# Transposes of the FFN activations: 32-bit float against the rounded 32-bit type, one unit later, in other PSUM banks

## What is computed

```python
hn = rms_norm(h, ffn_norm[i])
h = h + (jax.nn.silu(hn @ w_gate[i]) * (hn @ w_up[i])) @ w_down[i]     # D_FF = 5632
```

## Time and profile before

| | |
|---|---|
| median of 3 runs | 1308.03 us (1307.72 to 1308.03) |
| the profiled execution | 1307.81 us, its span 1306.1 us |
| TensorE busy | 1299.4 us (99%), granted clock at full speed throughout |
| VectorE busy | 1038.9 us (80%) |
| ScalarE busy | 713.9 us (55%) |
| bytes moved | 238 MB, mean 183 GB/s |

### The profile page before, as it was taken

How to read it: one execution, slowest core, us unless ns; L and a number is a source line. 1 busy time by engine, 2 the same in 40 slices (tenths; PEclk the granted TensorE clock), 3 DMA queues, 4 the chain that set the end, 5 groups by cost and what they waited for, 6 DMA issues and landing times.

```text
span 1306.1 us, 18433 instructions
## 1 busy us (share of the span) xinstructions
PE 1299.4 (99%) x6589; PEld 1073.9 (82%) x6589; DVE 1038.9 (80%) x1366; ACT 713.9 (55%) x946; POOL 57.1 (4%) x71
## 2 busy tenths in 40 slices
PE   9999999999999999999999999999999999999998
PEld 7788888888888888888888888888888888888887
DVE  6578885788586668999888977679888987968784
ACT  6576444544455556655455654445555545555753
POOL 5003000221000000000000000000000000000000
PEclk9999999999999999999999999999999999999999
DMA  8555544555444555766566656666666556657554
GB/s 272 177 177 162 160 148 130 146 147 148 144 128 145 178 177 162 219 216 185 184 200 204 204 188 208 187 211 188 195 208 211 188 181 210 191 178 221 181 180 162
DMA packets 126204, 238.37 MB, mean 183 GB/s; under 512 B 9711, under 2 KB 10786, under 8 KB 126138
## 3 DMA queue, kind: packets, MB, share of 16 engines
q1 hardware_dynamic: 126106, 237.48, 58.5%
q10 hardware_dynamic: 32, 0.01, 0.0%
HBM read 235.36 MB, written 2.10 MB: 182 GB/s over the span
## 4 chain that ended last, share of the span: by engine, by line
PE 97%; DVE 2%; ACT 0%; DMA 0%; issue 0%; DVEq 0%; ACTq 0%
PE pair L653 15%; PE pair L655 15%; PE pair L654 15%; PE pair L934 12%; PE pair L936 12%; PE pair L935 12%; PE bg L934 2%; PE bg L936 2%; PE bg L935 2%; PE bg L774 2%; PE bg L844 2%; PE bg L711 1%; PE bg L929 1%; DVE w_lo L1582 1%; PE bg L825 0%; PE bg L686 0%
## 5 line engine op out<-in xcount | busy, mean ns | idle before, releaser
L1582 DVE TENSOR_TENSOR w_lo<-raw,w_hi 128x1024 fp32r<-128x1024 f32 x442 | 532.8, 1222 | 163.8 <-ACT w_hi L1162 162.0
L1162 ACT ACTIVATE w_hi<-raw 128x1024 fp32r<-128x1024 f32 x399 | 415.3, 1055 | 246.5 <-PE pair L655 116.2
L653 PE MATMUL pair<-w_hi,xT_hi 128*128 128x512 f32 x716 | 289.5, 404 | 0.2 <-DVE w_lo L1847 0.2
L655 PE MATMUL pair<-w_hi,xT_lo 128*128 128x512 f32 x716 | 280.1, 391 | 0.0
L654 PE MATMUL pair<-w_lo,xT_hi 128*128 128x512 f32 x716 | 279.4, 390 | 0.0
L655 PEld LDWEIGHTS pair<-w_hi,xT_lo 128*128 128x128 f32 x716 | 134.4, 188 | 29.0
L653 PEld LDWEIGHTS pair<-w_hi,xT_hi 128*128 128x128 f32 x716 | 134.6, 188 | 27.1 <-issue 0.6
L654 PEld LDWEIGHTS pair<-w_lo,xT_hi 128*128 128x128 f32 x716 | 134.8, 188 | 24.7
L934 PE MATMUL pair<-w_hi,actT_hi 128*128 128x512 f32 x296 | 115.8, 391 | 0.0
L936 PE MATMUL pair<-w_hi,actT_lo 128*128 128x512 f32 x296 | 115.3, 390 | 0.0
L935 PE MATMUL pair<-w_lo,actT_hi 128*128 128x512 f32 x296 | 115.2, 389 | 0.0
(11 more groups left out here) (385 smaller groups left out, 1939.3 us busy)
## 6 DMA issues: line engine op xcount, KB each, us to landing
raw<-in_w_in_dram SPq DMA_DIRECT2D x112, 512.0 KB, 3.8
raw<-in_w_gate_dram SPq DMA_DIRECT2D x88, 512.0 KB, 4.2
raw<-in_w_up_dram SPq DMA_DIRECT2D x88, 512.0 KB, 4.2
raw<-in_w_down_dram SPq DMA_DIRECT2D x88, 512.0 KB, 4.8
raw<-in_w_o_dram SPq DMA_DIRECT2D x32, 512.0 KB, 4.5
raw<-in_w_ple_gate_dram SPq DMA_DIRECT2D x32, 512.0 KB, 4.8
raw<-in_w_ple_proj_dram SPq DMA_DIRECT2D x4, 512.0 KB, 4.4
h<-in_x_dram SPq DMA_DIRECT2D x3, 512.0 KB, 8.0
```

The costliest lines, as they stand in the source:

```text
L653: mm(banks[t][:], hi[:, ts], wh, start=first, stop=False)
L655: m = mm(banks[t][:], lo[:, ts], wh, start=False, stop=last)
L1162: f(w_hi[j % RING][:], raw[j % RING][:], ACT.Copy).then_inc(hi_ready, 1)
L1582: v.tensor_tensor(w_lo[j % RING][:], raw[j % RING][:], w_hi[j % RING][:].bitcast(F32), ALU.subtract).then_inc(lo_ready, 1)
```

## The change

The product of VectorE now goes to `gate_s` in place. ScalarE issues two DMAs that copy it, bits unchanged, into `act_r`, a tensor of the rounded type at the place of `act_s`. TensorE waits for their landing, transposes `act_r` against an identity of the rounded type (`ident_r`), and does so behind unit 3 instead of unit 2, into `bg[2]` and `bg[3]`. In `mixed_units` the product of `bg[2]` goes last and has the wait for `actT_lo`; `t_hi` and `t_lo` are made in pieces of 1 and 2 thirds instead of 2 and 1. The copying out of the banks stands behind the split of unit 6, outside `split_mixed`. `p1` is held in `v_s` instead of `act_s[1]`, and two VectorE instructions change places.

```diff
+TURN_BEHIND = 3
...
+        act_r = [sb(f"act_r{t}", [P, CB], F32R, at=mix + (52 + 2 * t) * KIB) for t in range(NT)]
...
+        ident_r = sb("ident_r", [P, P], F32R)
...
+            def tp_r(out, in_):
+
+                return nc.tensor.transpose(out.bitcast(F32R), in_, ident_r[:])
...
-            def turn_act():
-
-
+            def turn_act(n):
+
+                pe.wait_ge(ident_ready, 1)
+                for t in range(NT):
+                    pe.wait_ge(act_moved[t], n * 16)
                 for q in range(2):
                     for kk in range(2):
                         for t in range(NT):
                             cs = slice((2 * q + kk) * P, (2 * q + kk + 1) * P)
-                            m = tp(bg[q][:, kk * TOK + t * P:kk * TOK + t * P + P], act_s[t][:, cs], ident[:])
+                            m = tp_r(bg[2 + q][:, kk * TOK + t * P:kk * TOK + t * P + P], act_r[t][:, cs])
                     m.then_inc(ff_full[q], 1)
...
-                pe.wait_ge(t_lo_ready, n)
-                product(bg[2][:], F_hi[:, q, 2, :], F_lo[:, q, 2, :], t_hi[:, 1, :], t_lo[:, 1, :], first, last)
+                pe.wait_ge(t2_lo_ready, n)
                 product(bg[1][:], F_hi[:, q, 0, :], F_lo[:, q, 0, :], t_hi[:, 0, :], t_lo[:, 0, :], first, last)
-                pe.wait_ge(t4_lo_ready, n)
+                pe.wait_ge(t34_lo_ready, n)
                 product(pair[0][1][:], xT_hi[:, k1, a1], xT_lo[:, k1, a1], t_hi[:, 2, :], t_lo[:, 2, :], False,
-                        last).then_inc(t_used, 1)
+                        last)
+                if turned is not None:
+                    for f in range(2):
+                        pe.wait_ge(ff_free[f], turned)
+                product(bg[2][:], F_hi[:, q, 2, :], F_lo[:, q, 2, :], t_hi[:, 1, :], t_lo[:, 1, :], first, last).then_inc(t_used, 1)
...
-                            if not peeled:
-                                for n in range(2):
-                                    pe.wait_ge(ff_free[n], i + n0)
...
-                    if j == 2 and not peeled:
+                    if j == TURN_BEHIND and not peeled:
                         pe.wait_ge(pair_free[1], i * 2 + b0)
                         pe.wait_ge(gate_sum, i * 2 + 2 * n0)
-                        turn_act()
+                        turn_act(i + n0)
...
+            act.wait_ge(consts_ready, 1)
+            f(ident_r[:], ident[:], ACT.Copy).then_inc(ident_ready, 1)
             post("gains", 0)
...
-                f(t_hi[:, 0:2, :], t_raw[:, 0:2, :], ACT.Copy).then_inc(t_hi_ready, 1)
-                f(t_hi[:, 2, :], t_raw[:, 2, :], ACT.Copy).then_inc(t_hi_ready, 1)
+                f(t_hi[:, 0, :], t_raw[:, 0, :], ACT.Copy).then_inc(t_hi_ready, 1)
+                f(t_hi[:, 1:3, :], t_raw[:, 1:3, :], ACT.Copy).then_inc(t_hi_ready, 1)
...
+            def move_act(freed):
+
+                act.wait_ge(pair_free[1], freed)
+                for t in range(NT):
+                    act.dma_start(act_r[t][:].bitcast(F32), gate_s[t][:]).then_inc(act_moved[t], 16)
...
-                        split_mixed(u, j + LEAD, i * len(MIXED) + (m0 + q + 1), peeled and n0 == 0 and q == 0,
-                                    None if peeled or q else lambda: turned(i + (n0 - 1), i * 4 - 4))
+                        split_mixed(u, j + LEAD, i * len(MIXED) + (m0 + q + 1), peeled and n0 == 0 and q == 0)
                     else:
                         split(u, j + LEAD)
+                    if j == TURN_BEHIND and not peeled:
+                        turned(i + (n0 - 1), i * 4 - 4)
...
+                    if j == 0 and not peeled:
+                        move_act(i * 2 + b0)
                     if j == mixed_end:
                         act.wait_ge(t_used, i * len(MIXED) + (m0 + len(MIXED)))
-                        f(act_s[1][:], bg[0][:], ACT.Copy).then_inc(p1_copied, 1)
+                        f(v_s[:], bg[0][:], ACT.Copy).then_inc(p1_copied, 1)
...
-                v.tensor_tensor(t_lo[:, 0:2, :], t_raw[:, 0:2, :], t_hi[:, 0:2, :].bitcast(F32),
-                                ALU.subtract).then_inc(t_lo_ready, 1)
+                v.tensor_tensor(t_lo[:, 0, :], t_raw[:, 0, :], t_hi[:, 0, :].bitcast(F32),
+                                ALU.subtract).then_inc(t2_lo_ready, 1)
                 dve.wait_ge(t_hi_ready, 2 * n)
-                v.tensor_tensor(t_lo[:, 2, :], t_raw[:, 2, :], t_hi[:, 2, :].bitcast(F32),
-                                ALU.subtract).then_inc(t4_lo_ready, 1)
+                v.tensor_tensor(t_lo[:, 1:3, :], t_raw[:, 1:3, :], t_hi[:, 1:3, :].bitcast(F32),
+                                ALU.subtract).then_inc(t34_lo_ready, 1)
...
-                        v.tensor_tensor(v_s[:], bg[1][:], p1[:], ALU.subtract).then_inc(v_ready, 1)
-                        v.tensor_tensor(gate_s[0][:], pair[0][0][:], p1[:], ALU.add).then_inc(gate_sum, 1)
+                        v.tensor_tensor(gate_s[0][:], pair[0][0][:], v_s[:], ALU.add).then_inc(gate_sum, 1)
+                        v.tensor_tensor(v_s[:], bg[1][:], v_s[:], ALU.subtract).then_inc(v_ready, 1)
...
-                            v.scalar_tensor_tensor(out=act_s[t][:], in0=up[:], scalar=h_rs[0][:, t:t + 1],
+                            v.scalar_tensor_tensor(out=gate_s[t][:], in0=up[:], scalar=h_rs[0][:, t:t + 1],
```

More of the change, by code:

```diff
@@ L382, in build @@
         h1_copied = sem("h1_copied")
+        act_moved, ident_ready = [sem(f"act_moved{t}") for t in range(NT)], sem("ident_ready")
         act_copied, act_form, act_rounded, down_sum = (
@@ L387, in build @@
         t1_ready, t2_ready, t34_ready = (sem(f"t{n}_ready") for n in (1, 2, 34))
[L388 to L389 removed]
+        t_hi_ready, t2_lo_ready, t34_lo_ready, t_used = (
+            sem(n) for n in ("t_hi_ready", "t2_lo_ready", "t34_lo_ready", "t_used"))
         p1_copied, gate_sum, v_ready, up_sum = (
@@ L936, in product, with mixed_units @@
                 return mm(o, lo, wh, start=False, stop=last)
-            def mixed_units(u, j, q, n):
+            def mixed_units(u, j, q, n, turned=None):
                 first, last = q == 0, q == len(MIXED) - 1
@@ L1046, in down @@
                                     False).then_inc(unit_used, 1)
-                            pe.wait_ge(t_lo_ready, count)
-                            product(bg[2][:], D_hi[:, q, 2, :], D_lo[:, q, 2, :], t_hi[:, 1, :], t_lo[:, 1, :], first, last)
+                            pe.wait_ge(t2_lo_ready, count)
                             product(bg[1][:], D_hi[:, q, 0, :], D_lo[:, q, 0, :], t_hi[:, 0, :], t_lo[:, 0, :], first, last)
-                            pe.wait_ge(t4_lo_ready, count)
+                            pe.wait_ge(t34_lo_ready, count)
                             product(pair[0][1][:], actT_hi[:, k1, a1], actT_lo[:, k1, a1], t_hi[:, 2, :], t_lo[:, 2, :], False,
-                                    last).then_inc(t_used, 1)
+                                    last)
+                            product(bg[2][:], D_hi[:, q, 2, :], D_lo[:, q, 2, :], t_hi[:, 1, :], t_lo[:, 1, :], first, last).then_inc(t_used, 1)
                             continue
@@ L1107, in _ @@
                             False).then_inc(unit_used, 1)
-                    pe.wait_ge(t_lo_ready, MIX_PG + q + 1)
-                    product(bg[2][:], E_hi[:, q, 3, :], E_lo[:, q, 3, :], t_hi[:, 1, :], t_lo[:, 1, :], first, last)
+                    pe.wait_ge(t2_lo_ready, MIX_PG + q + 1)
                     product(bg[1][:], E_hi[:, q, 1, :], E_lo[:, q, 1, :], t_hi[:, 0, :], t_lo[:, 0, :], first, last)
-                    pe.wait_ge(t4_lo_ready, MIX_PG + q + 1)
+                    pe.wait_ge(t34_lo_ready, MIX_PG + q + 1)
                     product(pair[0][1][:], xT_hi[:, k1, a1], xT_lo[:, k1, a1], t_hi[:, 2, :], t_lo[:, 2, :], False,
-                            last).then_inc(t_used, 1)
+                            last)
+                    product(bg[2][:], E_hi[:, q, 3, :], E_lo[:, q, 3, :], t_hi[:, 1, :], t_lo[:, 1, :], first, last).then_inc(t_used, 1)
                     continue
@@ L1443, in split_mixed @@
                 f(w_hi[j % RING][:], raw[j % RING][:], ACT.Copy).then_inc(hi_ready, 1)
-                if between:
-                    between()
                 if not n0_first:
@@ L1533, in _ @@
                     gate_up(i, ug, bgt, n0, False, mg)
-                down(ud, n, n0, md)
+                down(ud, bd, n, n0, md)
             for u in range(U_PP, UNITS):
@@ L1901, in turned, with split_mixed @@
                     ks = bass.ds(kt + 2 * q, 2)
-                    v.tensor_tensor(actT_lo[:, ks, :], bg[q][:].rearrange("p (k n) -> p k n", k=2),
+                    v.tensor_tensor(actT_lo[:, ks, :], bg[2 + q][:].rearrange("p (k n) -> p k n", k=2),
                                     actT_hi[:, ks, :].bitcast(F32), ALU.subtract).then_inc(ff_free[q], 1)
-            def split_mixed(u, j, n, first, between):
+            def split_mixed(u, j, n, first):
                 jg, ju = (j - 1) % RING, j % RING
```

(5 more changed lines are left out.)

25 lines of the change are left out of this document (12 added, 13 removed).

## The result

| | before | after |
|---|---|---|
| median | 1308.03 us (1307.46 to 1309.38, 13 runs) | 1310.93 us (1310.13 to 1311.49, 13 runs) |
| profiled execution, its span | 1307.81, 1306.1 us | 1310.31, 1308.6 us |
| one trip of the gate/up loop | 42.40 us | 42.72 us |
| a turn (what TensorE gives to eight transposes) | 0.884 us | 0.705 us |
| `w_lo` of unit 4 starts, after the end of the last multiply | 1.05 us | 2.45 us |

The ratio is 1.002, with an interval of 1.0012 to 1.0029. The change makes the kernel **slower by 0.2%**. The prediction said 1305.7 with a range of 1303.6 to 1308.9, so the result lies outside it, on the other side of no change.

A forecast was written before the change was run, and what follows sets the result against it. It took TensorE, busy 99% of the span, as the bound. Nine trips x (0.36 saved - 0.18 stall) = 1.6, plus 0.7 in the down stages, made 2.3 less than 1308.03: 1305.7 us, range 1303.6 to 1308.9.

The forecast's parts named there:

- What bounds the kernel: Whole kernel: TensorE busy for 99% of the span, so only less TensorE work saves time; VectorE, busy 38.82, is next.
- Rounded transposes at 0.057: TensorE's turns: each rounded transpose takes 0.057 instead of 0.109, saving 0.36 us a turn, 4.0 over eleven.
- load and stream overlap in part: Rival on TensorE's turns: 0.084 a transpose, 0.71 a turn, no stall, 1.9 less, 1306.1; chance 0.08.
- ScalarE's issues at 0.37: ScalarE behind unit 3's split: two DMA issues of 0.37 each make w_lo of unit 4 1.0 us late.
- the rival without a stall: ScalarE's issue is shorter or the shift absorbed, so all eleven turns count: 4.0 less, 1304.0; chance 0.25.
- The stall model: Up unit of the third mixed pair: TensorE waits 0.18 a trip for late w_lo, half of the trip's gain.
- the issue on ScalarE: Rival: an issue takes 0.82, the third pair stalls 1.08, 5.8 more, 1313.8; chance 0.08.
- a cover of 2 to 4: Turn behind unit 3: copies land 2 to 4 us before TensorE wants them, costed at nothing.
- the 0.7: bank 2's product: activation copies end near 684.1, the product writing their bank starts at 684.8; cover 0.7, no cost.
- The moves at nothing: Turn moved behind unit 3, 2.73 us later, with later copies and reordered VectorE work: costed at nothing.
- Further traffic at nothing: DMA engines, 63% busy: the added 22 x 256 KB costed at nothing.
- The down stages kept both turns: Down stages: ScalarE waits 2 us there anyway, so two turns x 0.36 = 0.7 us are all kept.

The follow-up runs named there:

- the kernel with SP's issues: The changed kernel with SP issuing both copies in the loops, ahead of its eighth weight load, instead of ScalarE: 1306.37 us, ratio 0.9984.
- The kernel with plain copies: The changed kernel with the same DMAs into a plain tensor and plain float32 transposes: 1310.80 us, ratio 1.0018.
- the order alone: The changed kernel without DMAs and with plain float32 transposes, keeping the later place, other banks and new order: 1308.33 us, ratio 0.9999.
- a third issue: The changed kernel with a third, 16 KB DMA issued by ScalarE behind the two: 1316.71 us, ratio 1.0063.
- one DMA: The changed kernel with both halves copied by one DMA of 512 KB instead of two: 1306.45 us, ratio 0.9985.
- three issues behind unit 4: The changed kernel with a third, 16 KB DMA, all three issued in the loop behind unit 4's split instead of unit 3's: 1306.30 us, ratio 0.9985.

## Why the prediction was wrong

**What bounds the kernel.** Right: less work for TensorE or a new wait were the two ways, and VectorE was the neighbour to watch. But "there is a wait of 0.4 us for a landing at the start", and no other, was read from TensorE's matmuls alone. The list of waits of the weight loads has more, for the kernel before:

```profile
PEld pair L934 <- DVE w_lo L1582: 1.4, 2, 0.7
```

Those are two mixed pairs of a first, peeled block (the product at 522.39 starts 0.67 behind the one ahead of it, which started at 521.72). Two loads of plain units wait for `w_lo` as well, 0.5 together. VectorE was already late where the pairs lie, twice. It costs the change nothing, but it was a sign that the pairs have little cover.

**Rounded transposes at 0.057: wrong, and the first term that was mis-sized.** They take 0.083, between the bounds, so 2.0 instead of 4.0 for eleven turns. The half that was wrong is the load: the trace has 0.082 to 0.086 from load to load, against the 0.06 of the prediction. The streaming half, 0.057, was right; it shows in the first distance of a turn, where the load is done ahead. The 0.06 was read from how much longer two loads last than one in the earlier trace rows, for a tensor on 32 partitions in plain float32. The two transposes of that row themselves start 0.084 apart in the single records (67.668 and 67.752), though they have only 32 moving columns, and that was there to be read. Why one type of load takes 0.083 and the other 0.11 stays open. The rival "load and stream overlap in part" had 0.084 and 0.71, and a chance of 0.08. Its size was hit to 0.001 and 0.005 by luck: 0.084 was the middle of two bounds and came from no row, and by the records of the loads it is no partial overlap, but the load alone that sets the pace. The figure named beside that rival, in the Trainium skill, "TensorE: Matmul & The Clock Gate", Back-to-back issue gap (about 81 ns for a load and product of 128 columns in a stream), agrees with the 0.083; ordinary products in this type, at 0.11, do not come to it. The same page's factor of four for transposes of FP32 (Terms), by which a transpose would take 0.055, does not agree: the rows give 2 for plain float32, and a transpose in the rounded type is 0.22 / 0.083 = 2.7 times as fast as a plain float32 product.

**ScalarE's issues at 0.37: wrong, and the term that decided.** They take 0.47 and 0.62. The resume came out right otherwise: first issue 0.03 behind the multiply, 0.19 from the last issue to `w_hi` where I had 0.16. So `w_lo` of unit 4 was 1.40 late and not 1.0. The 0.37 was SP's, for loads of weights; SP takes 0.38 for those in the kernel with SP's issues and 1.13 for this pair. The row that fitted by engine, 0.46 for ScalarE's one issue at the start, is the value of the first issue here (0.47). I had written that 0.50 an issue is where the gain ends and 0.64 where it shows as slower; that was for transposes at 0.057, and the measured mean is 0.55. Two of my arguments here don't stand up to the trace of before. That every issue takes 0.37 or more, put against the rival without a stall, is not so: SP issues the small rows of the start in 0.25 to 0.41 and the last stores in 0.33 and 0.34. And against long issues I had put that the loop's take 0.37, but those are loads issued one at a time; six loads of weights that SP issued directly behind another DMA took 0.43 to 0.49.

**The stall model: right in its mechanism, a little small.** It had waits of 0.18 at a delay of 1.0, at the up unit of the third pair. With the delay at 1.40 and the turn only 0.18 shorter, the same sum gives 0.18 + 0.40 - 0.18 = 0.40, where 0.46 was measured, and the place is as said, but for 0.05 at the second pair. The delay that TensorE can bear is 0.9. Putting both measured terms into the prediction: 9 x (0.40 - 0.18) - 2 x 0.18 = 1.6 more instead of 2.3 less. The 0.9 that is missing to the measured 2.5 is 0.06 of waits and 0.04 of wider distances in each trip. The issue alone turns the sign: with transposes at 0.057 the stall is 0.58, and 9 x (0.58 - 0.36) - 0.7 = 1.3 more, little better than with both. The transposes alone do not: at 0.083 with a delay of 1.0 there is no stall (0.18 - 0.18), and 2.0 less. The kernel with plain copies says the same from the other side.

**The range and the chances.** The issue's bounds were "from small to 0.46", though the same group of rows had 0.82 and though no row showed two issues directly behind one another on ScalarE; 0.82 was left to a rival with 0.08. That is the step that failed in the numbers: the price of the two issues, 0.37 each and at most 0.46, where the runs show 0.47 and 0.62. "Overlap in part" and "the issue on ScalarE" were also priced each with the other at the forecast's value, and the sizes of both came, in part or in full: they are about different engines, so nothing kept them apart.

**What held.** The landing in 2.6 us of a cover of 2 to 4: no wait at the turn. No wait at `bg[2]`'s product, with 0.44 of cover left of the 0.7 (a wait appears only with a third issue). The moves at nothing (the order alone: 1308.33). Further traffic at nothing (the issues on SP). The down stages kept both turns: the budget closes only with their -0.36. The waits for `w_lo` in the third mixed pair came in each of the nine trips, "about 0.2" being about 0.4.

## What to carry to other kernels

Issuing a DMA is work of the engine whose list it stands in: price it from a row of the same engine and the same kind of transfer, and then ask what stands behind it in that list, since here the same two issues cost 4.6 to 5.0 us ahead of a `w_hi` that VectorE was waiting for and nothing one place later. When TensorE gets faster and another engine later in one change, find the delay that the loop can bear (here 0.9 us, the mixed pairs' slack), because beyond it the loop runs at the late engine's pace and the saving on TensorE is not paid out. Price the rivals in pairs as well, where they are about different engines.

## What the runs showed of the hardware

- A pair of 256 KB copies within on-chip memory took 0.47 + 0.62 us to issue on ScalarE and 0.49 + 0.60 on SP; one of 512 KB took 0.47, and a third of 16 KB 0.62 (0.54 to 0.63 over the trips). So the first issue took 0.47 to 0.54 over all trips, and the second 0.60 to 0.63 in nearly all; 256 or 512 KB made no difference to the first, and 16 KB was not shorter behind two others. A weight load of 512 KB, alone, took SP 0.37 to 0.38. Why a copy takes longer than a load and the second longer than the first, no run shows. The Trainium skill, "DMA: Bandwidth & Descriptors", Issuing engines are not separate DMA queues, calls the time to initiate a DMA usually small relative to the DMA itself; here it was 1.1 us for a pair whose landing took 2.6 us from the issue, and it is what decided.
- 128 columns against the identity stand 0.109 apart as plain float32 transposes, 0.083 as rounded transposes, and 0.11 as ordinary rounded products: the type alone gives nothing, the transpose in that type does. In the two rounded forms the weight loads stand as far apart as the products (0.082 to 0.086, 0.108 to 0.112), while the first distance, with the load done ahead, is 0.057 to 0.062 in both: 128 columns stream faster than they are loaded.
- A late weight operand shows up as waiting of the weight load more than of the product: in after, the products' list has 0.4 us of waits for `w_lo` (2 times, none in the loops), the loads' list 7.8 us (19 times).
- Between kernels whose trips are all 42.21 to 42.23 long there remain some tenths (1305.78 to 1306.54). In the profiled executions they lie ahead of the first turn: with the issues on SP, one DMA, three issues behind unit 4, two there and one there, the first turn starts at 553.75, 553.57, 553.38, 553.18 and 552.85, and from there to the end all five take 751.13 to 751.17. They are no effect of where or how the copies are issued in the loop, and what makes them isn't explained here.
